# Experts' tokens modulated and split once, gathered as a rounded part and a rest; five rounding buffers for six

## The reference, cut to what matters

```python
h = modulate(x, sh2, sc2)          # rms_norm(x) * (1 + scale) + shift
logits = h @ router_w + router_b   # [256, 8]
top_vals, top_idx = lax.top_k(logits, 2)
combine = one_hot(top_idx) weighted by softmax(top_vals)
for e in range(8):
    y = (silu(h @ w_gate[e]) * (h @ w_up[e])) @ w_down[e]
    out = out + combine[:, e:e + 1] * y
x = x + g2 * out
```

## Time and profile before

| | |
|---|---|
| median of 3 runs | 3048.66 us (3047.83 to 3050.3) |
| the profiled execution: its time | 3049.76 us |
| the profiled execution: its span | 3047.6 us |
| PE busy | 2860.0 us, 94% of the span |
| DVE busy, ACT busy | 1878.1 us, 1573.9 us |
| granted TensorE clock, mean | 0.969 |
| moved by DMA | 693.76 MB, mean 228 GB/s |

### The profile page before, as it was taken

One profiled execution on the slowest core, in us unless ns is written; L12 is line 12 of the kernel. 1 busy time (PEld: TensorE's weight loads), 2 busy tenths in 40 slices (PEclk: granted clock), 3 DMA queues, 4 the chain that ended last, 5 costly groups with the idle time before them and its releaser, 6 DMA issues. The chain is left out here.

```text
span 3047.6 us, 37628 instructions
## 1 busy us (share of the span) xinstructions
PE 2860.0 (94%) x14894; PEld 2316.9 (76%) x14895; DVE 1878.1 (62%) x1975; ACT 1573.9 (52%) x1792; POOL 19.2 (1%) x45
## 2 busy tenths in 40 slices
PE   7999899999899999999999999979998998999898
PEld 4788798778777878778787787857556986746697
DVE  3766454575597988879888798833503551531454
ACT  3574443566377777767777776732312441321343
POOL 0000000000000000000000000010000000000000
PEclk9999899899899999999999999989999999999999
DMA  9755553855678989899998999844232444313351
GB/s 336 250 189 184 194 180 112 304 171 177 228 256 329 366 326 370 328 344 349 325 370 328 362 333 330 303 159 147 79 122 99 166 161 144 117 49 138 115 197 70
DMA packets 311099, 693.76 MB, mean 228 GB/s; under 512 B 7238, under 2 KB 26164, under 8 KB 310980
## 3 DMA queue, kind: packets, MB, share of 16 engines
q1 hardware_dynamic: 309024, 689.07, 62.7%
q0 software_dynamic: 1344, 2.82, 0.5%
q10 hardware_dynamic: 612, 0.18, 0.0%
HBM read 690.99 MB, written 1.05 MB: 227 GB/s over the span
## 5 line engine op out<-in xcount | busy, mean ns | idle before, releaser
L2239 DVE TENSOR_TENSOR ring_rest<-ring,weights_hi 128x2048 fp32r<-128x2048 f32 x270 | 605.1, 2284 | 34.3 <-ACT weights_hi L1710 33.4
L1710 ACT ACTIVATE weights_hi<-ring 128x2048 fp32r<-128x2048 f32 x270 | 514.3, 1920 | 125.1 <-PE ps L1492 78.8
L1490 PE MATMUL ps<-weights_hi,xg_hi 128*128 128x512 f32 x1008 | 402.8, 400 | 3.5 <-DVE xg_lo L2239 3.5
L1492 PE MATMUL ps<-weights_hi,xg_lo 128*128 128x512 f32 x1008 | 395.8, 393 | 0.0
L1710 ACT ACTIVATE arena<-ps 128x512 f32<-128x512 f32 (+6 forms) x311 | 160.2, 531 | 415.3 <-PE ps L1118 137.7
L1491 PE MATMUL ps<-ring_rest,xg_hi 128*128 128x512 f32 x792 | 310.6, 392 | 0.0
L1509 PE MATMUL ps<-weights_hi,hidden_split_moe 128*128 128x512 f32 x1008 | 281.9, 391 | 0.0
L1710 ACT ACTIVATE arena<-arena 128x256 f32<-128x256 f32 (+5 forms) x240 | 136.8, 596 | 264.6 <-DVEq L2299 65.5
L2239 DVE TENSOR_TENSOR w_split<-ring,w_split 128x1024 fp32r<-128x1024 f32 x128 | 151.0, 1221 | 168.4 <-ACT w_split L1710 168.4
L2239 DVE TENSOR_TENSOR late_rest<-arena,weights_hi 128x2048 fp32r<-128x2048 f32 x108 | 244.5, 2284 | 6.2 <-ACT weights_hi L1710 4.3
L1710 ACT ACTIVATE weights_hi<-arena 128x2048 fp32r<-128x2048 f32 x108 | 207.8, 1924 | 64.9 <-PE ps L1492 34.9
(11 more groups left out here) (244 smaller groups left out, 4759.6 us busy)
## 6 DMA issues: line engine op xcount, KB each, us to landing
ring<-in_moe_w_gate_dram SPq DMA_DIRECT2D x54, 2048.0 KB, 7.9
ring<-in_moe_w_up_dram SPq DMA_DIRECT2D x45, 2048.0 KB, 7.9
ring<-in_moe_w_down_dram SPq DMA_DIRECT2D x36, 2048.0 KB, 7.8
ring<-in_mlp_w_dram SPq DMA_DIRECT2D x32, 2048.0 KB, 8.4
arena<-in_moe_w_down_dram SPq DMA_DIRECT2D x27, 2048.0 KB, 8.0
ring<-in_w_mod_dram SPq DMA_DIRECT2D x48, 1024.0 KB, 9.1
ring<-in_w_in_dram SPq DMA_DIRECT2D x48, 1024.0 KB, 5.4
arena<-in_moe_w_up_dram SPq DMA_DIRECT2D x18, 2048.0 KB, 7.9
```

The source lines that it names most:

```text
L1490: pe.matmul(b, xg_hi[:, k, :], hi[:, i, :], start=(k == 0), stop=False)
L1492: mm = pe.matmul(b, xg_lo[:, k, :], hi[:, i, :], start=False, stop=(k == KD - 1))
L1710: return act.activation(o, i, func, **kw)
L2239: return dve.tensor_tensor(o, a, b, op)
```

## The change

`xn_moe` goes. The transposed, modulated tokens `hT`, made for the router anyway, are transposed back once (four groups of four transposes), rounded by ScalarE into `tokens_hi` and subtracted by VectorE into `tokens_lo`. A turn then gathers each of the two, in float32r, 16 products of 128x128 each: the rest first, into the two accumulator banks, then the rounded part. `to_slots` is float32r too. A 0/1 matrix moves values unchanged, so ScalarE copies `xg_hi` out of PSUM (two ACTIVATEs of 128x512) and VectorE copies `xg_lo` (two of 128x512); the modulation, the rounding and the subtraction in each turn go. `tokens_lo` takes the room of one weight buffer: HI_BUFFERS is 5, and the buffer of piece p is `HI_OF[p]`, five in rotation with the order turned by one after blocks 1, 3 and 5.

```diff
-HI_BUFFERS = 6
+HI_BUFFERS = 5
+def rounded_in():
+    order, buffers = list(range(HI_BUFFERS)), []
+    for block in range(-(-2 * 3 * GROUPS // HI_BUFFERS)):
+        buffers += order
+        if block in (1, 3, 5):
+            order = order[1:] + order[:1]
+    return buffers[:2 * 3 * GROUPS]
+HI_OF = rounded_in()
+def last_in_buffer(p):
+    return next(q for q in range(p - 1, p - 4 * HI_BUFFERS, -1) if HI_OF[q % len(HI_OF)] == HI_OF[p])
...
+            for i in range(2 * TT):
+                b = open_bank(("tokens", i))
+                for n in range(4):
+                    mm = pe.transpose(b[:, n * P:(n + 1) * P],
+                                      hT[:, 4 * (i % 2) + n, (i // 2) * P:(i // 2 + 1) * P], ident)
+                done(mm)
...
-                for half in range(2):
-                    b = open_at(lambda i: ("gather", i, half), e)
+                for n in range(4):
+                    tokens, half = (tokens_lo if n < 2 else tokens_hi), n % 2
+                    if n == 0:
+                        pe.wait_ge(sem("to_tokens_ready"), 1 + e)
+                        pe.wait_ge(acc_emptied, base_acc + e)
+                        pe.wait_ge(sem("tokens_rest_ready"), 1)
+                    b = acc(1, half) if n < 2 else open_at(lambda i: ("gather", i, half), e)
                     for i in range(4):
                         k = 4 * half + i
                         for t in range(TT):
-                            mm = pe.matmul(b[:, i * P:(i + 1) * P], xn_moe[:, t, k * P:(k + 1) * P],
-                                           to_slots[:, t], start=(t == 0), stop=(t == 1))
+                            mm = pe.matmul(b[:, i * P:(i + 1) * P], tokens[:, t, k * P:(k + 1) * P],
+                                           to_slots[:, t], start=(i == 0 and t == 0), stop=(i == 3 and t == 1))
...
-                pe.wait_ge(sem("xg_split_ready"), 1 + e)
+                pe.wait_ge(sem("xg_rest_ready"), 1 + e)
+                pe.wait_ge(emptied["act"], nth_at(lambda i: ("gather", i, 1), e))
...
+            for i in range(2 * TT):
+                b = full(act, ("tokens", i))
+                f(tokens_hi[:, i // 2, (i % 2) * 512:(i % 2 + 1) * 512], b, ACT.Copy).then_inc(sem("tokens_rounded"), 1)
...
-                    act.wait_ge(pe_done, piece_done(p - HI_BUFFERS, e))
-                    f(weights_hi[:, p % HI_BUFFERS], piece_cols(slot_mem(s), p), ACT.Copy)\
+                    act.wait_ge(pe_done, piece_done(last_in_buffer(p), e))
+                    f(weights_hi[:, HI_OF[p]], piece_cols(slot_mem(s), p), ACT.Copy)\
...
+            for i in range(2 * TT):
+                dve.wait_ge(sem("tokens_rounded"), i + 1)
+                at = slice((i % 2) * 512, (i % 2 + 1) * 512)
+                empty(tt(tokens_lo[:, i // 2, at], bank(("tokens", i)), tokens_hi[:, i // 2, at].bitcast(F32),
+                         ALU.subtract), ("tokens", i))
+            dve.wait_ge(emptied["dve"], taken[0])
+            dve.sem_inc(sem("tokens_rest_ready"), 1)
             dve.wait_ge(sem("top_weights"), 1)
...
-                b = bank(("gather", 0, 1))
-                for i in range(4):
-                    k = 4 + i
-                    ins = ts(xg[:, k], b[:, i * P:(i + 1) * P], scale[:, k:k + 1], ALU.mult,
-                             shift[:, k:k + 1], ALU.add)
-                ins.then_inc(emptied["dve"], 1)
+                for half in range(2):
+                    ins = dve.tensor_copy(xg_lo[:, 4 * half:4 * half + 4].rearrange("p k n -> p (k n)"), acc(1, half))
+                ins.then_inc(sem("xg_rest_ready"), 1)
                 add_scattered(0)
                 add_scattered(1)
-                dve.wait_ge(sem("xg_rounded"), 1 + e)
-                tt(xg_lo[:, :, :], xg, xg_hi[:, :, :].bitcast(F32), ALU.subtract).then_inc(sem("xg_split_ready"), 1)
```

More of the change, by code:

```diff
@@ L232, in __init__ @@
                 self.add(("rt",), "dve")
+                for i in range(2 * TT):
+                    self.add(("tokens", i), "dve")
                 self.add(("pos",), "dve")
@@ L302, in experts @@
         for e in range(TURNS):
-            self.add(("gather", e, 0), "act")
-            self.add(("gather", e, 1), "dve")
+            for i in range(2):
+                self.add(("gather_rest", e, i), "acc")
+            for i in range(2):
+                self.add(("gather", e, i), "act")
             for i in range(2 * TT):
@@ L604, in program @@
         hidden_split_moe = rounded("hidden_split_moe", free_at, 2, 512)
-        xn_moe = expert.cut(TT, D)
-        to_slots = expert.cut(TT, P)
+        tokens_at = expert.pos
+        expert.cut(TT, D)
+        tokens_hi = rounded("tokens_hi", tokens_at, TT, D)
+        to_slots = rounded("to_slots", expert.pos, TT, P)
+        expert.cut(TT, P)
         weighted = expert.cut(TT, P)
@@ L616, in program @@
         weights_hi = rounded("weights_hi", hi_at, HI_BUFFERS, 2048)
+        tokens_lo = rounded("tokens_lo", expert.pos, TT, D)
+        expert.cut(TT, D)
         ring_rest = nc.alloc_sbuf_tensor_at("ring_rest", [P, RING_A, SLOT], F32R,
@@ L835, in program @@
         turn_steps = value["moe_gate", 1, 0] - value["moe_gate", 0, 0]
-        turn_empties = {who: plan.nth["gather", 1, i] - plan.nth["gather", 0, i]
-                        for i, who in enumerate(("act", "dve"))}
+        turn_empties = {who: plan.nth[kind, 1, 0] - plan.nth[kind, 0, 0]
+                        for who, kind in (("act", "gather"), ("dve", "scatter"))}
         def nth_at(key_of, e):
@@ L951, in load_turn @@
                         sp.wait_ge(sem("lru_dir_done"), 2 * L)
-                        sp.wait_ge(sem("xn_ready"), 2 * L)
+                        sp.wait_ge(pe_done, value["tr2", 1, 3])
                     what, g = expert_slots()[i]
@@ L1385, in _ @@
                 mix_out(l, (merged_hi, merged_lo))
-                turn("tr2", l, xn if l == 0 else xn_moe, "xn_ready", 2 * l + 2)
+                turn("tr2", l, xn, "xn_ready", 2 * l + 2)
                 hT_ready("tr2", l)
@@ L2061, in expert_turn @@
                     round_piece(p)
[L2062 to L2070, removed]
+                for half in range(2):
+                    act.wait_ge(pe_done, step_at(lambda i: ("gather", i, half), e))
+                    f(xg_hi[:, 4 * half:4 * half + 4].rearrange("p k n -> p (k n)"), bank(("gather", 0, half)), ACT.Copy)\
+                        .then_inc(emptied["act"], 1)
                 for p in range(4, HI_BUFFERS):
@@ L2602, in _ @@
                 add_branch(("wo", l), gb[:, 0], tmp1)
-                normed(x, xn if l == 0 else xn_moe, "xn_ready")
+                normed(x, xn, "xn_ready")
                 if l == 0:
@@ L2749, in expert_turn @@
                 gated_y(piece_done(-1, e))
[L2750 to L2756 removed]
+                dve.wait_ge(pe_done, step_at(lambda i: ("gather_rest", i, 1), e))
+                for half in range(2):
+                    ins = dve.tensor_copy(xg_lo[:, 4 * half:4 * half + 4].rearrange("p k n -> p (k n)"), acc(1, half))
+                ins.then_inc(sem("xg_rest_ready"), 1)
                 add_scattered(0)
                 add_scattered(1)
[L2759 to L2760 removed]
                 add_scattered(2)
```

12 lines of the change are left out of this document (5 added, 7 removed).

## The result

| | before | changed |
|---|---|---|
| median | 3048.68 us (6 runs, 3047.83 to 3050.3) | 3066.03 us (6 runs, 3058.64 to 3067.05) |
| ratio, 95% interval | | 1.0051 (1.0038 to 1.0064) |
| the profiled execution: span, mean granted clock | 3047.6 us, 0.969 | 3064.9 us, 0.965 |

The account below looks back on a forecast made before the run. TensorE's list of products was taken to bound each turn. Entry 1.0 plus stalls 13.5 less split 4.0 gave +10.5 us (9.7 with 0.6 gained a turn), taken as 10 on 3048.7: 3058.7 us, range 3044 to 3070.

Parts of the forecast that it names:

- Five buffers: Mid-turn, down 0 and down 2: hidden copies queued behind waiting roundings stall TensorE 0.75 us each, 13.5 us in nine turns.
- The split: Start of each turn: the 0.40 us wait ahead of piece 0 goes, 0.5 us a turn, 4 us gained.
- The gather: Start of each turn: 32 products at 0.118 us, 3.7 us again; up to 4.33 us costs nothing, scatter waits for `y_slots`.
- The rival of a slow product: Gather: a 128-column float32r product takes 0.229 us, gather 7.3 us, 27 us in nine turns, 3085.7 us; chance 0.13.
- The entry: Ahead of the first turn: VectorE's added subtractions delay the gather; piece 0 at 856.5 against 855.51, 1.0 us lost.
- The delay of VectorE's chain: Ahead of the first turn: four subtractions of 0.64 us before the weights make the COPY, and so the gather, 1.6 us later.
- ends 5.65 later ... 3.55 us on, piece 0 starts: First turn: gather ends 5.65 us after its start, at 852.97; piece 0 starts 3.55 us on, at 856.5.
- The part behind the turns: After the last turn: the prediction had no term for it, forecasting nothing.
- the likeliest case: Whole kernel: 3058.7 us, by itself 3054 to 3063 with stalls of 0.6 to 0.9 us; chance 0.58.
- one stall: Mid-turn: only one of the two stalls comes, or both half as long; +3 us, 3052 us; chance 0.10.
- a slower product: Gather: the range takes in a product of up to 0.16 us; each 0.01 above 0.135 costs 2.9 us.
- The rival on the other side: Down 0 and down 2 find hidden values in time, leaving only gain and entry; -3 us, 3045.7 us; chance 0.15.

Follow-up runs that it names:

- e1: Changed kernel with the order of the five buffers turned after blocks 0, 5 and 6 instead of 1, 3 and 5; 3049.95 us, ratio 1.0001.
- e5: Kernel before with the change's five buffers and their order, old gather, split and entry kept; 3066.57 us, ratio 1.0062.
- e2: Changed kernel with the order of the five buffers turned after blocks 2, 3 and 7; 3073.84 us, ratio 1.0083.
- e3: Changed kernel with ScalarE's rounding at the second gate half moved behind that group's hidden copy; 3047.93 us, ratio 0.9997.
- e4: Changed kernel's gather with six buffers in plain rotation, tokens' rest left out so values are not the block's; 3049.11 us, ratio 0.9999.
- e6: Changed kernel with the 16 gather products of the rest issued twice in each turn; 3076.35 us, ratio 1.0088.
- e7: e3 with 32 more transposes of 128x128 on TensorE ahead of the first turn, result never read; 3049.55 us, ratio 1.0002.
- e9: Kernel before with 13 more transposes of 128x128 ahead of each turn's gather; 3061.00 us, ratio 1.0029.
- e11: Kernel before with only VectorE making `y_slots` before the rest of piece 1; 3051.51 us, ratio 1.0001.
- e8: e7 with VectorE making `y_slots` before the rest of piece 1; 3036.25 us, ratio 0.9968.

## Why the prediction was right, and where it was off

- **Five buffers: right in mechanism and size.** Forecast two stalls of 0.75 us a turn, at down 0 and down 2, none at down 4. Measured 0.74 (the change against e1), 0.73 (e5 against before); two waits a turn; e2 makes three of them, e1 and e3 none. That the cause is the place in ScalarE's queue and not the stock is shown from both sides.
- **The split: right, a little small.** Forecast 0.5 us a turn gained, measured 0.64 (e4).
- **The gather: right.** Forecast 0.118 us a product and no effect on the scatter; measured 0.108, with the wait for `y_slots` 0.65 us still there. The rival of a slow product is out. The Trainium skill's "TensorE: Matmul & The Clock Gate" has two figures that bear on it: some 81 ns for load and product in "Back-to-back issue gap", which this trace doesn't bear out for float32r, and columns over 1.2 GHz for a load in "LDWEIGHTS (loading the stationary operand)", 107 ns for 128, which it does.
- **The entry: the term that was mis-sized.** Forecast 1.0 us, measured 3.6, or 3.2 counted from `tr2`. The delay of VectorE's chain was right to 0.1 us on that count. The step that failed is "ends 5.65 later ... 3.55 us on, piece 0 starts": it carried over the lengths of gather and scatter from before, where the clock rose in mid-gather. In the changed kernel it stayed low until within the scatter, as in all runs whose float32r gather starts at the low clock, e6 with its longer one included; the cause behind that stays open. e7 shows that the gather takes 3.8 us where the clock is high.
- **The part behind the turns: forecast nothing, measured 5.4 us** in the profiled execution. The two executions at 0.969 have 10 to 12 us for the whole change (3058.64, 3060.98), near the sum of the prediction. Neither was profiled, but e2 and e5, profiled at 0.969, have 1.7 less and 0.2 us more than before in this part. That the sum comes so near is partly luck: an entry 2.2 us dearer than forecast stands against turns 1.2 us cheaper. The median of 3066.03 lies above the 3054 to 3063 given for the likeliest case and inside the range, which was wide for other reasons (one stall, a slower product); no term of it stood for this clock. The 17.4 us of the medians are the entry, the turns and the clock behind the turns. e9 and e11 give the same low clock with other edits, one that lengthens the turns and one that shortens them. It is therefore not owed to the change's instructions; what decides in an execution whether it comes wasn't found, and stays open.
- **The rival on the other side** (no late copies, -3 us) is what e1 and e3 are: in the turns it gives 0.64 us each, and the entry takes it back.

## What to carry to other kernels

Before taking a buffer away, look at what is queued behind the instruction that will wait for it, not only at whether the stock suffices: here the stock did, and the loss was a copy of 0.6 us locked in behind a rounding; which pieces are near mattered, not how many. Removing work from engines that aren't the bound gave only the one wait that it ended (0.64 us a turn), and the order of two VectorE steps gave 0.34 in the kernel before but 0.82 on top of the shorter split: two waits in a row are best removed together. A term taken over from a trace at one clock holds only where the clock is the same. Where a kernel's executions fall into groups by granted clock, compare within a group: a median can move by 5 us without the edit having done it, and e11's gain is hidden in one.

## What the runs showed of the hardware that wasn't expected

- A float32r product of 128 columns with its own 128x128 weights comes every 0.108 us at the full clock, hardly faster than a float32 record of the same size (0.118), although one of 256 columns comes every 0.122.
- TensorE's clock fell at 852.7 us behind the idle 1.63 us of e7 (granted 1.00 from 847 to 852 us, 0.66 from 852 to 857), and stayed at 1.00 in e8, where that wait is gone. In e7 and e8 it also fell, at 842.5 and 842.9, while TensorE had been at work since 840.1 and 840.7.
- The clock rose 3.8 to 4.7 us behind the start of the float32 products of 128 columns of before, e5, e9 and e11, and of the transposes of e7 and e8. It didn't rise in a float32r gather of 6.9 us, nor in e6's of 10.3 us, with TensorE busy 11.87 of 12 us at 0.50, nor in the router's float32 products of 8 columns (6.97 us from 828.83 in the kernel before, at 0.50). The same gather took 3.8 or 7.1 us for it, the scatter 3.6 to 5.4.
